# Stick-breaking attention on one core: the transposes of a token tile move from the middle of the next tile's projection to a place behind the value products

## The reference, cut to what matters

```python
q, k, v, g = jnp.split(h @ w_in, 4, axis=-1)          # 16 heads of 64
z = einsum('bqhd,bkhd->bhqk', q, k) * (B_DH ** -0.5)
valid = k_pos[None, :] < q_pos[:, None]
log_keep = where(valid, log_sigmoid(-z), 0.0)
after = cumsum(log_keep, axis=3, reverse=True) - log_keep
a = where(valid, exp(log_sigmoid(z) + after), 0.0)
o = einsum('bhqk,bkhd->bqhd', a, v)
o = o.reshape(b, t, B_WIDTH) * silu(g)
return o @ w_out, k, v
```

## Time and profile before

| what | value |
|---|---|
| median of 3 runs | 2052.14 us (2051.48 to 2052.67) |
| the profiled execution's own time | 2052.41 us |
| its span, first to last instruction | 2050.3 us |
| TensorE matmul (PE) busy | 1908.9 us, 93% of the span |
| VectorE (DVE) busy | 1126.9 us, 55% |
| ScalarE (ACT) busy | 1069.3 us, 52% |
| GpSimd (POOL) busy | 387.1 us, 19% |
| mean granted TensorE clock | 0.975 |

### The profile page before, as it was taken

One profiled execution on the slowest core, in us unless ns is written; L12 is line 12 of the kernel. 1 busy time (PEld: TensorE's weight loads), 2 busy tenths in 40 slices (PEclk: granted clock), 3 DMA queues, 4 the chain that ended last, 5 costly groups with the idle time before them and its releaser, 6 DMA issues. The chain is left out here.

```text
span 2050.3 us, 35228 instructions
## 1 busy us (share of the span) xinstructions
PE 1908.9 (93%) x11429; PEld 1634.9 (80%) x11429; DVE 1126.9 (55%) x2269; ACT 1069.3 (52%) x2556; POOL 387.1 (19%) x597
## 2 busy tenths in 40 slices
PE   4999999999999899986899999999999999989996
PEld 4888878878878699985777777777777777689995
DVE  5547456465564622554275757575657575754455
ACT  5455455454564521453375657575757575732335
POOL 0133132221331000453010101010101011100341
PEclk9999999999999999998999999999999999999999
DMA  4121121112211252212010101010101010233213
GB/s 152 57 63 36 46 60 56 50 47 57 62 36 47 96 141 66 64 65 73 21 58 27 57 26 57 26 57 26 57 26 57 26 57 26 96 111 97 62 44 131
DMA packets 161746, 124.18 MB, mean 61 GB/s; under 512 B 10992, under 2 KB 152624, under 8 KB 161648
## 3 DMA queue, kind: packets, MB, share of 16 engines
q1 hardware_dynamic: 160784, 122.85, 19.7%
q10 hardware_dynamic: 864, 0.20, 0.0%
HBM read 89.49 MB, written 33.52 MB: 60 GB/s over the span
## 5 line engine op out<-in xcount | busy, mean ns | idle before, releaser
L107 PE MATMUL pj<-area,h_high 128*128 128x384 f32 (+1 forms) x2304 | 666.6, 352 | 26.7 <-DVE lb_qk_low L1360 6.5
L107 PEld LDWEIGHTS pj<-area,h_high 128*128 128x128 f32 (+1 forms) x2304 | 413.6, 184 | 49.1 <-DVE lb_qk_low L1360 7.9
L107 PE MATMUL pj<-area,h_low 128*128 128x384 f32 (+1 forms) x1152 | 394.0, 342 | 0.0
L107 PEld LDWEIGHTS pj<-area,h_low 128*128 128x128 f32 (+1 forms) x1152 | 213.1, 185 | 8.7
L1532 POOL TENSOR_TENSOR lb_o<-lb_o,lb_keep 128x512 f32<-128x512 f32 (+3 forms) x80 | 77.1, 964 | 630.8 <-ACT lb_keep L1232 624.2
L1377 DVE SCALAR_TENSOR_TENSOR lb_s<-lb_sc,lb_m 128x512 f32<-128x512 f32 (+4 forms) x200 | 110.0, 550 | 85.1 <-ACT lb_m L1213 85.1
L1203 ACT ACTIVATE lb_m<-lb_sc 128x512 f32<-128x512 f32 (+4 forms) x200 | 89.1, 488 | 103.9 <-PE lb_sc L1614 41.5
L456 ACT ACTIVATE la_p<-la_sc,la_nm 128x128 f32<-128x128 f32 (+5 forms) x144 | 105.7, 737 | 33.7 <-DVE la_nm L653 32.8
L1408 DVE CAST lb_s_high<-lb_s 128x512 fp32r<-128x512 f32 (+1 forms) x192 | 109.0, 568 | 25.1
L1410 DVE TENSOR_TENSOR lb_s_low<-lb_s,lb_s_high 128x512 fp32r<-128x512 f32 (+1 forms) x192 | 114.6, 597 | 6.6
L651 DVE TENSOR_REDUCE la_mx<-la_sc 128x1 f32<-128x128 f32 (+5 forms) x144 | 107.6, 747 | 2.9
(11 more groups left out here) (307 smaller groups left out, 4470.1 us busy)
## 6 DMA issues: line engine op xcount, KB each, us to landing
stage<-in_a_w_in SPq DMA_DIRECT2D x60, 192.0 KB, 3.0
stage<-in_b_w_in SPq DMA_DIRECT2D x60, 192.0 KB, 2.6
stage<-in_ple_w_gate SPq DMA_DIRECT2D x22, 512.0 KB, 3.9
h_low<-o_t SPq DMA_DIRECT2D x14, 528.0 KB, 6.5
mix_b_xs<-x_mid SPq DMA_DIRECT2D x8, 528.0 KB
lift_xt<-in_x SPq DMA_DIRECT2D x8, 512.0 KB, 4.7
stage<-in_a_w_in SPq DMA_DIRECT2D x16, 256.0 KB, 5.2
out_ak<-la_tok SPq DMA_DIRECT2D x8, 512.0 KB, 3.3
```

The lines of the kernel that those rows point to most:

```text
L107: last = pe.matmul(out, x, y, start=start and n == 0, stop=stop and n == 2, **kw)
```

## The change

In TensorE's program of `stick_layer` all nine `turn` calls of a pass leave the middle of a projection (or gate piece) and stand directly behind `values(i - 2)`, ahead of `after(i - 1)`. Turns 0 to 3 turn the tiles 5 to 8, turns 8 to 12 the tiles 0 to 4 of the next group: the same tile in the same turn as before. The other engines' programs, the prologue ahead of the first pass and the other stages are unchanged.

```diff
                     if i >= 2:
                         values(i - 2)
+                    if i < 4:
+                        turn(at, i + 5)
+                    if more and 8 <= i <= 12:
+                        turn(ahead, i - 8)
                     if i >= 1:
                         for s in units(i - 1):
                             after(s)
...
                         project(at, t, 0)
-                        turn(at, t - 1)
                         project(at, t, 1)
...
                     if i in GATE_AT:
                         gate_project(GATE_AT[i], 0)
-                        if i == 3:
-                            turn(at, NT)
                         gate_project(GATE_AT[i], 1)
...
                             project(ahead, t, 0)
-                            turn(ahead, t - 1)
                             project(ahead, t, 1)
                         if i == 12:
                             free_bank(5)
                             project(ahead, 5, 0)
-                            turn(ahead, 4)
                         if i == 13:
                             project(ahead, 5, 1)
```

## The result

The changed kernel takes 2040.14 us (median of 5 runs, 2038.89 to 2043.13), the kernel before, timed beside it, 2052.14 (2051.36 to 2053.38): a ratio of 0.9943, 95% interval 0.9929 to 0.9957. That is 12.0 us faster. The forecast was 5.5 us, and 2043.0 to 2050.0 as the range; the time lies under it. A second timing gave 2039.82 us and a ratio of 0.9932 (0.9919 to 0.9945). Executions of one kernel spread: in the largest set the kernel before took from 2047.0 to 2055.3 us over 35 runs.

What follows compares the result with a forecast made beforehand. PE's own order was taken as the bound, with one idle gap in turn 1. Terms of 1.6 (tile 6), 1.7 (tile 8) and 2.2 us (43 pairs) summed to 5.5: 2052.14 to 2046.6 us, range 2043.0 to 2050.0.

Steps and rivals of the forecast that it cites:

- The 43 pairs: Transposes of tile 7 and tiles 0 to 4, moved between value and triangle products: 0.05 us gained each, 2.2 us.
- tile 8: Its 32-row transposes leave the middle of a gate piece for turn 3: 0.21 us gained in eight passes, 1.7 us.
- tile 5's gain: Its pair moves behind `scores(0)` in turn 0, ahead of PE's idle time in turn 1: gain 0.
- The pair of tile 6: Moves into PE's idle time in turn 1: seven passes at 0.22 us, the first at 0.05, 1.6 us.
- the hole: PE's idle time in turn 1 of passes 2 to 7, triangle products waiting for VectorE's low halves: 25.6 us in 26 times.
- The rival in which the 43 gain nothing: Only tiles 6 and 8 count, 3.3 us: 2048.8 us; chance 0.23 together with the case of half of tile 8's gain.
- a step of 0.10 us still standing behind the first triangle product: Sign of being wrong: the triangle product's open load of 0.10 us still paid with the pair ahead of it.
- The new wait: Each moved pair waits for `tok_ready` with less work to cover the copy; 0.8 us in hand at tile 8, cost 0.
- The copies come too late: Rival: each pair waits, though 0.7 to 0.8 us are in hand; chance 0.06 together with more falls of the clock.
- the clock falls less often: Rival: two fewer 3.4 us stretches at clock 0.50, 1.7 us each, giving 2043.2 us; chance 0.09.
- another number of stretches at 0.50: Sign of being wrong: the count of stretches with the clock at 0.50 differs from before.
- the slower rival: The clock falls more often, behind turn 1's idle time and the sample's scores, 1.7 us each; chance 0.06 with late copies.

Runs made afterwards that it cites:

- tile 6 alone: Against the kernel before, only tile 6's pair of transposes moves, the other pairs stay in the projections: 2051.25 us, ratio 0.9990.
- the others alone: The changed kernel with tile 6's pair put back between the halves of tile 7's projection: 2050.72 us, ratio 0.9995 to the kernel before.
- the kernel with the hole filled: The changed kernel with tile 7's projection moved into PE's idle time of turn 1, tile 5's q and k copied first in the pass: 2010.12 us, ratio 0.9794.

## Why the prediction was wrong

*The pairs.* Right in size in each term that can be read by itself. The 43 pairs save 0.05 us each, 2.0 us against 2.2; tile 8 saves 0.22 against 0.21; tile 5's gain is a few hundredths. The pair of tile 6 is hidden in the hole, with the copy landing 0.7 us ahead of the triangle product; its 0.22 can be read apart from the clock only where turn 1 has the same falls at nearly the same moments, in the passes 4 and 8: 0.14 and 0.19 us shorter. The rival in which the 43 gain nothing is out: 0.17 us was measured for a pair, not 0.22. By the Trainium skill's rule on loads (TensorE: Matmul & The Clock Gate, "LDWEIGHTS (loading the stationary operand)") a pair would have cost 0.22 behind the value products, too; the trace disagrees, with 0.17.

The way to the 0.05 is less sure than its size. The prediction took a step of 0.10 us still standing behind the first triangle product as a sign of being wrong, and 0.09 stand there (0.26 against 0.17 in turn 2). But behind a pair inside a projection the same 0.26 stood before the change (1212.31 to 1212.57 in the earlier trace rows), within the 0.22 that the pair was priced at, so this sign could not tell the cases apart. What is shown is the whole stretch, 0.45 us against 0.28; its split into open loads is not.

*The new wait* costs nothing: its 7.8 us lie in the hole, where the earlier trace rows had VectorE's wait alone. *The copies come too late*: in none of the changed kernel's turns but turn 1 does PE wait for them.

*The step that failed* is the clock, in the sum itself. The prediction entered the falls at zero in the likeliest case, and gave "the clock falls less often", as two falls fewer, a chance of 0.09, since "these places come at other moments". The runs show a term with a sign: 12.0 us less the 5.5 of the priced terms leaves 6.5. The stretches at 0.50 went from fifteen to nine and eleven in two executions (51 us to 31 and 38); at the prediction's 1.7 us for each that is up to 10 and 7 us. So the price of a fall was about right (turn 1 of the passes 3 and 6 lost 1.8 and 1.7 us with one stretch each, the pair's gain within), the number of them was not, and another number of stretches at 0.50 was one of its own signs of being wrong. The rival that came about had the right direction; its two falls were a guess. That pair and length work on each other was not thought of: tile 6 alone 1.1 us, the others alone 1.6, together 12.0 to 12.6. The prediction did say that the pair makes the hole shorter, but used it only against the slower rival. A hint stood in the rows: the clock is low behind the hole with PE busy again, and behind the sample's scores it falls in one pass and not in the next, at the same work. That the hole brings about the low clock behind it, the rows could not show; the kernel with the hole filled and the passes 1 and 8 do.

*What stays open*: how the length of a pass decides. The runs show that it does where the hole is broken or filled (0.32 us more per pass costs 7.8 and 6.8 us, 0.48 less gains 14), and that it does much less where the hole is whole (0.64 us more costs 3.2) or the pass is shorter still. They do not show which length is good beforehand, and no figure here foretells the next one. Falls also feed back on the length: in the changed kernel a pass that falls at both places takes 102.0 to 102.6 us and one without a fall 98.8, so a fall moves the moments of all later passes. Whether that settles which passes fall, no run tests. Why there is a hole stays open, too: ahead of its first two steps ScalarE stands 2.24 and 1.79 us in "issue" in pass 2 of the kernel before, and not at all in the passes 1 and 8, the ones that do not follow a jump back of the loop.

## What to carry to other kernels

Before pricing an edit near an idle gap of TensorE, look at the granted clock in the windows behind that gap in every pass: if it falls there in any pass, the edit's own price is not the answer, and the range must hold the case that all of those falls go or come. When a change moves the time by more than its parts, run each part alone, run the whole again, and then change the loop's length by work that has nothing to do with it; that told a coupling from luck here. And fill such a gap with the loop's own work rather than trim beside it: the projection in the hole was worth 30 us more than the change.

## What the runs showed of the hardware that was not expected

With sixteen transposes (1.9 us) in the hole the clock stayed at 1.00 behind it in all six passes, with 1.5 us of products in two of six; the two kernels differ in the length of the pass as well, so that comparison is not clean. A pass about as much shorter with an empty hole, that of all pairs but tile 6's, fell in all six. With the hole filled, the clock stayed at 1.00 for 749 us in the one execution that was profiled, the stretch of small score products in each pass included, behind which it had fallen in 5 of 8 passes before.
